# The SSM diagonal stage without its matmuls into tiles that are written again at once

## The reference, cut to what matters

```python
Lmat = segsum_exp(a)          # exp(cs_l - cs_s), lower triangle of each chunk, else 0
y_diag = jnp.einsum('bclgn,bcsgn,bgrcls,bcsgrp->bclgrp', Cc, Bc, Lmat, xd)
...
y_f = ssd_scan(xs, dt_f, A[0], Bm, Cm)
y_b = flip(ssd_scan(flip(xs), flip(dt_b), A[1], flip(Bm), flip(Cm)))
y = y_f + y_b + xs * d_skip.astype(jnp.float32)[:, None]
```

## Time and profile before

| | |
|---|---|
| three executions | 3081.49 to 3083.79 us, median 3082.02 us |
| profiled execution, own time | 3093.99 us |
| its span | 3092.1 us |
| mean granted TensorE clock | 0.975 |
| TensorE busy | 2972.6 us (96%) |
| VectorE busy | 1702.5 us (55%) |
| ScalarE busy | 1023.8 us (33%) |
| GpSimd busy | 207.6 us (7%) |
| DMA | 248.61 MB, mean 80 GB/s |
| instructions | 34121, 13945 of them matmuls |
| L1319 | 60 matmuls, first at 493.9 us, last at 575.3 us |

### The profile page before, as it was taken

The page is one execution under the profiler, slowest core; times in us unless marked ns, Lnnn a source line. Parts: engine busy times, 40 slices in busy tenths (PEclk is TensorE's granted clock), DMA queues, the critical chain, the costliest instruction groups (busy, mean ns, idle before and its releaser), DMA issues.

```text
span 3092.1 us, 34121 instructions
## 1 busy us (share of the span) xinstructions
PE 2972.6 (96%) x13945; PEld 2356.9 (76%) x13945; DVE 1702.5 (55%) x1994; ACT 1023.8 (33%) x1503; POOL 207.6 (7%) x151
## 2 busy tenths in 40 slices
PE   6899999999999999999998999999799999999999
PEld 5567776767768788888866888788686878888887
DVE  7777866655583333333367766676637433343435
ACT  2213336513241121121245555556524311121212
POOL 3420011162000000000000000000000000000000
PEclk7899999999999999999999999999799999999999
DMA  6455465015211111111130111112121311111203
GB/s 205 138 184 164 157 204 210 29 58 206 67 34 48 48 48 48 47 49 46 55 123 26 34 45 50 41 41 65 38 95 41 123 32 44 48 61 34 68 28 136
DMA packets 261687, 248.61 MB, mean 80 GB/s; under 512 B 7022, under 2 KB 234831, under 8 KB 261519
## 3 DMA queue, kind: packets, MB, share of 16 engines
q1 hardware_dynamic: 248518, 194.00, 20.3%
q0 software_dynamic: 12000, 48.61, 4.2%
q10 hardware_dynamic: 1040, 4.19, 0.3%
HBM read 213.55 MB, written 41.09 MB: 82 GB/s over the span
## 4 chain that ended last, share of the span: by engine, by line
PE 89%; DVE 6%; ACT 2%; issue 1%; DMA 0%; POOL 0%; SPq 0%; ACTq 0%; DVEq 0%; POOLq 0%
PE psum_gemm L217 14%; PE psum_gemm L218 14%; PE psum_gemm L221 14%; PE psum_misc L1761 8%; PE psum_gemm L2108 7%; PE psum_misc L217 4%; PE psum_misc L218 4%; PE psum_misc L221 4%; PE psum_gemm L320 3%; PE psum_misc L2172 3%; PE psum_gemm L2193 3%; PE psum_gemm L2181 2%; PE psum_misc L828 1%; DVE ada_w L492 1%; PE psum_gemm L2194 1%
## 5 line engine op out<-in xcount | busy, mean ns | idle before, releaser
L217 PE MATMUL psum_gemm<-h_hi,w_hi 128*128 128x512 f32 x1968 | 782.4, 398 | 21.1 <-POOL h_lo L403 10.1
L218 PE MATMUL psum_gemm<-h_lo,w_hi 128*128 128x512 f32 x1968 | 769.5, 391 | 0.0
L221 PE MATMUL psum_gemm<-h_hi,w_lo 128*128 128x512 f32 x1968 | 608.8, 391 | 0.0
L217 PEld LDWEIGHTS psum_gemm<-h_hi,w_hi 128*128 128x128 f32 x1968 | 371.3, 189 | 120.9 <-issue 34.3
L221 PEld LDWEIGHTS psum_gemm<-h_hi,w_lo 128*128 128x128 f32 x1968 | 371.2, 189 | 78.3
L218 PEld LDWEIGHTS psum_gemm<-h_lo,w_hi 128*128 128x128 f32 x1968 | 371.5, 189 | 77.1 <-issue 2.9
L1825 ACT ACTIVATE w_hi<-w_raw 128x1024 fp32r<-128x1024 f32 x108 | 113.9, 1056 | 374.7 <-PE psum_gemm L221 184.7
L199 ACT ACTIVATE w_hi<-w_raw 128x1024 fp32r<-128x1024 f32 x79 | 83.2, 1055 | 444.2 <-PE psum_gemm L221 314.9
L1937 DVE TENSOR_SCALAR gate_act<-gate_in,params 128x1024 f32<-128x1024 f32 x44 | 35.8, 813 | 321.8 <-ACT gate_in L1872 321.5
L1872 ACT ACTIVATE gate_in<-psum_gemm 128x1024 f32<-128x1024 f32 x42 | 43.3, 1030 | 477.1 <-PE psum_gemm L221 477.1
L1761 PE MATMUL psum_misc<-down_w,ffn_act_hi 128*128 128x512 f32 x704 | 188.4, 389 | 2.5 <-DVE ffn_act_lo L1959 2.5
(11 more groups left out here) (350 smaller groups left out, 4873.0 us busy)
## 6 DMA issues: line engine op xcount, KB each, us to landing
w_raw<-in_f_w_up SPq DMA_DIRECT2D x88, 512.0 KB, 3.8
ada_w<-in_w_ada SPq DMA_DIRECT2D x40, 1024.0 KB, 5.4
w_raw<-in_f_w_down SPq DMA_DIRECT2D x44, 512.0 KB, 3.4
w_raw<-in_e_w_in SPq DMA_DIRECT2D x29, 512.0 KB, 6.5
w_raw<-in_o_w_qkv SPq DMA_DIRECT2D x24, 512.0 KB, 3.9
ada_w_first<-in_w_ada SPq DMA_DIRECT2D x4, 2048.0 KB, 19.8
w_raw<-in_e_w_out SPq DMA_DIRECT2D x16, 512.0 KB, 4.8
skew_scratch<-bias_scratch POOLq DMA_DIRECT2D x1, 7680.0 KB, 49.8
```

The source lines that it names most:

```text
L217: pe.matmul(o, wh, rh[:, k, c], start=(k == 0), stop=False)
L218: pe.matmul(o, wh, rl[:, k, c], start=False, stop=False)
L221: last = pe.matmul(o, wl, rh[:, k, c], start=False, stop=(k == nk - 1))
```

## The change

The loop of L1318 runs eight times for heads 0 and 1 as before, and no longer at all for heads 2 to 15. This takes out 28 matmuls (14 heads, two directions) with their weight loads. Nothing is added or moved; all waits and signals stay where they are, and what is computed is the same.

```diff
@@ -1315,7 +1315,7 @@
                         scores_pe(pe, 0)
                     if h >= 1:
                         pe.wait_ge(s_exp, 2 * h - 1 + d)
-                    for n in range(8 if h < 2 else 1):
+                    for n in range(8 if h < 2 else 0):
                         pe.matmul(pG[:, d, n % 2 * HALF:(n % 2 + 1) * HALF], identR[:],
                                   maskR[:, d:d + 1].to_broadcast([P, 4, P]), start=True, stop=True)
                     if h == d == 0:
```

## The result

The changed kernel took 3128.60, 3132.71, 3133.20 and 3084.96 us, median 3130.65; the kernel before beside it 3082.9 us median (3081.49 to 3090.28, 4 executions). The change made the kernel slower, by 46 to 50 us in three of four executions. I had forecast 3075.9 us.

What follows compares the result with a forecast made beforehand. The stage was taken as bound by TensorE's queue, then by its mutual waits with ScalarE. Savings of 5.2 us in steady heads and 0.94 in early ones, 6.1 together, took 3082.02 to 3075.9 us; range 3072.0 to 3083.5.

Steps and rivals of the forecast that it cites:

- What bounds the stage: In the steady heads TensorE's queue sets the 4.88 us period, with ScalarE 0.65 us behind, waiting for L1328.
- The worth of a removed matmul: TensorE's queue saves 0.23 us in direction 1 and 0.28 in direction 0, together 0.51 us per head.
- the ring: TensorE and ScalarE waiting on each other: 8.82 us per two heads, 4.41 per head, saving 0.47 us a head.
- neither 4.37 nor 4.23: Periods in us that would refute 4.41: TensorE's queue alone gives 4.37, ScalarE's own work 4.23.
- The sum: Steady heads 4 to 15 save 11 x 0.47 = 5.2 us, early heads 0.94, together 6.1 us.
- the 0.43 of head 3: Head 3, direction 1: without L1319, L1324 starts at ScalarE's signal, saving 0.43 us.
- rival 3: Gain absorbed later by an engine bound to absolute time in a later stage; about 3082 us, chance 0.10.
- The clock: TensorE's full clock would hold in the stage, with a pause of only 0.04 us per head.
- The price: A low-clock stretch of 3.5 us costs at most 1.7 us of TensorE's time.
- Rival 2: Clock falls in heads 4 to 15; gain gone from four low stretches, 3087.8 us with half low; chance 0.12.
- The chance of 0.08 for slower: Chance that the whole kernel gets slower by over 0.2%, all from the clock falling in the stage.
- The Trainium skill's rule: A kernel whose TensorE paused briefly and often between matmul groups had its clock swing between levels; it spoke against the change.

Runs made afterwards that it cites:

- only_3: Changed kernel with one unused matmul per block kept in head 3 alone; 3081.21 us against 3086.96 before, ratio 0.9984.
- fill_2to4: Changed kernel with one unused matmul per block kept in heads 2 to 4; 3082.27 us against 3087.22 before, ratio 0.9987.
- burst_8: Changed kernel plus eight unused matmuls in the first block of head 8; 3094.93 to 3105.37 us, ratio 1.0047.
- fill_5on: Changed kernel with one unused matmul per block from head 5 on; six executions, 3089.17 to 3146.72 us.
- fill_6on: Changed kernel with one unused matmul per block from head 6 on; 3086.73 and 3133.12 us.
- only_4: Changed kernel with one unused matmul per block in head 4 alone; seven executions 3076.20 to 3087.84 us, five 3128.44 to 3137.00.
- pause_67: Kernel before, all unused matmuls kept, with TensorE waits added in heads 6 and 7; 3137.46 us against 3083.72, ratio 1.0166.
- thin_2to4: Changed kernel with one 128-column unused matmul per block in heads 2 to 4; seven executions 3080.20 to 3087.29 us, three 3125.38 to 3133.11.

## Why the prediction was wrong, point by point

- *What bounds the stage* held: from head 4 on ScalarE waited for L1328 in every head, before and after.
- *The worth of a removed matmul* and *the ring* held, where the clock did. In only_3 the period is 4.41 us, as forecast, with 0.15 to 0.20 us in front of each start where 0.18 was expected, and neither 4.37 nor 4.23. The change from the y products to the 64-row matmul takes its place as in the earlier trace rows: in only_3 L1324 starts 0.07 us before the products end (516.27 + 2.00 = 518.27, start 518.20).
- *The sum* held for what it describes. In the trace of only_3 the steady part takes 48.52 us instead of 53.73, 5.2 less, as forecast. Only_3, which keeps two of the 28, should save 6.1 less the 0.43 of head 3, 5.7 us, and is 5.75 us below the kernel before by the medians; fill_2to4 should save 5.2, the steady part alone, and saves 4.95. By the intervals these are 2.5 to 7.7 and 0.9 to 7.4 us, so that they agree to a few tenths is luck. The saving does reach the end, at least in part, and rival 3 in full does not occur.
- One reading was wrong: the last of the 32 L1319 starts at 506.5 us, not near 504.6. No other number hangs on it.
- *The clock* is the step that failed, and with it the forecast. The place: I looked for it in heads 4 to 15 and weighed the pause per head there, 0.04 us. It fell in head 3, where my own sum had a row with L1319 behind a wait for ScalarE (516.12) and counted it as 0.43 us saved. That saved time became a wait, 0.25 + 0.43 = 0.68 us, and TensorE is busy only 3.33 of the 4.00 us from 514 to 518, at the end of which the clock falls. The steady part, which I priced, holds its clock without any filler.
- *The price* failed too. Rival 2 had 1.7 us per low stretch of 3.5 us, as though each ended by itself, because the rows of before show short ones. Here one fall was one low stretch of 109.2 us and cost some 40 us, since at 1.2 GHz a head takes 7.91 us instead of 4.41 and nothing in the stage lifted the clock. "From four such stretches on" should have read "from the first one on". I never asked what the stage looks like once it is low: TensorE's 16 products grow from 1.90 to 3.51 us, ScalarE's 16 exponentials only from 4.23 to 4.47, and the same matmuls are spread over nearly twice the time.
- The chance of 0.08 for slower, and the range's end of 3083.5, followed from both errors.
- *The Trainium skill's rule* in "TensorE: Matmul & The Clock Gate", section "A second HAM failure mode: psum-queue depth-cycling", pointed the right way, and I held the trace at full clock against it. The runs agree in so far as the clock fell where a wait had grown from 0.25 to 0.68 us, but the picture is not a swing between the levels: it is one fall and no return for 109.2 us. The same page's section "Why this matters for your kernels" advises to keep TensorE busy continuously to get to the full clock; here it was busy 105.00 of 105.00 us at 0.50 by the profile, and what brought the clock up was the burst in burst_8 and, in the changed kernel, the matmuls of the next stage, at 627.0 us. The measurement decides.

What stays open: why one execution falls and the next does not. Up to the y products of head 3 the code is the same in the changed kernel, burst_8, fill_5on, fill_6on and only_4, and all eight profiles of them have the same wait of about 0.68 us there; four fell and four did not. Here is one that did not, fill_6on:

```profile
516.41 0.73 PE L1324 MATMUL psum_gemm<-cs_rows,sel_r 64*128 64x512 f32 x2 [0.68 <-ACT decays L1355]
517.06 0.73 PE L1328 MATMUL psum_gemm<-mask_r,ident_r 128*128 128x512 f32 x2
517.72 0.31 PE L1044 MATMUL psum_misc<-ident,ada_part 40*128 40x40 f32 x2
517.97 2.00 PE L1304 MATMUL psum_misc<-x_S,chunk_weights 128*128 128x64 f32 x16
```

So the wait alone does not decide. What does part the eight is how the work lies to an earlier change of the clock. Every profile has a short low stretch just ahead of the heads or as they begin (490.46 to 493.88 us in the changed kernel, 492.54 to 495.96 in fill_6on). From its end to the start of the y products of head 3 it is 22.5 to 22.9 us in the four that fell (516.35 - 493.88 = 22.47 in the changed kernel) and 21.8 to 22.1 us in the four that did not (517.97 - 495.96 = 22.01 in fill_6on). The kernel before, with its fillers, lies among the fallen ones by this measure (518.12 - 495.60 = 22.52) and held its clock. This is read from nine traces and was not tested.

Open too: why the lower heap of the changed kernel (3084.96 to 3093.27 us) is not 6 us below the kernel before. None of its four executions was profiled. In the two unfallen profiles of fill_5on the first exponential of the stage comes late, at 501.2 us against 498.1 in the kernel before and 497.0 in the three fallen profiles of the changed kernel, so that those that do not fall may be those that come late to the stage; but fill_6on (498.6) and only_4 (498.1) did not fall either, and burst_8 (498.3) did.

## What to carry to other kernels

Before unused matmuls are taken out, look for the few microseconds around them in which the engine does least, above all those behind a wait, and not at the mean of the stage; one or two kept there can be worth more than the rest together cost. Price a fall of TensorE's clock by whether the work that follows can lift it again: work out the period of the stage at 1.2 GHz, and count with the chance that it stays there for the whole remaining stage, as it did here. Run such a change many times and read the executions one by one, since the same program can fall or not.

## What the runs showed of the hardware that was not expected

- The low clock can outlast a long stretch of steady work: one low stretch of 109.2 us in the changed kernel, with TensorE busy in 105.00 of the 105.00 us from 522 to 627, and one of 105.8 us in pause_67. Both ended only in the next stage.
- The level has a memory. The same head without fillers runs at 4.41 us and 2.4 GHz in only_3, and at 7.91 us and 1.2 GHz in the changed kernel; which one is decided near 518 us. With a filler per block the two are 4.88 and 8.87 us.
- Eight 512-column matmuls in a row (3.76 us) ended it in burst_8; one more per block did not in pause_67, nor did the 16 narrow products of 3.51 us in each head.
- Whether it falls differs from execution to execution of one program (14 of 18 for the changed kernel, 5 of 12 for only_4, 3 of 10 for thin_2to4), and the same wait of 0.68 us stands in profiles that fell and in profiles that did not.
